# Attention in a two-block transformer kernel: probabilities divided on GpSimd and turned in transpose mode, scores on 64 rows of q and k

## The reference

```python
# layer 0: latent queries over all keys and values; the context queries over the context alone
s = einsum('bqkgd,btkd->bkgqt', qblk, k) * scale
p = softmax(s, axis=-1)
o = einsum('bkgqt,btkd->bqkgd', p, v)
# layer 1: keys within 128 positions plus all context keys, and a logit per head (the sink) in the softmax
p = softmax(concatenate([where(mask, s_w, -inf), s_c, s_sink], axis=-1))
# last layer: all keys up to the query's own chunk, with a bias by relative position
p = softmax(where(valid, scores + bias, min))
```

## Time and profile before

| | us |
|---|---|
| median of 3 runs | 3030.41 (3017.93 to 3030.89) |
| the profiled execution | 3029.36 |
| its span | 3027.6 |
| TensorE busy | 2899.5 (96%) |
| VectorE busy | 1686.7 (56%) |
| GpSimd busy | 1145.4 (38%) |
| ScalarE busy | 1050.2 (35%) |
| attention of layer 0 | 191.7 to 333.7 |
| attention of layer 1 | 1136.5 to 1326.3 |
| attention of the last layer | 2227.4 to 2295.6 |

### The profile page before, as it was taken

How to read it: one execution, slowest core, us unless ns; L and a number is a source line. 1 busy time by engine, 2 the same in 40 slices (tenths; PEclk the granted TensorE clock), 3 DMA queues, 4 the chain that set the end, 5 groups by cost and what they waited for, 6 DMA issues and landing times.

```text
span 3027.6 us, 43720 instructions
## 1 busy us (share of the span) xinstructions
PE 2899.5 (96%) x15898; PEld 2441.1 (81%) x15898; DVE 1686.7 (56%) x2794; ACT 1050.2 (35%) x1926; POOL 1145.4 (38%) x782
## 2 busy tenths in 40 slices
PE   8889999999999979999999999999999979899998
PEld 6779878888888769987888878888788758688886
DVE  5577886555545667775555564444544674432223
ACT  3247332111111437753222242222354673222222
POOL 1333223333333153323554544544353324334443
PEclk8989999999999999999999999999999999999999
DMA  5100333323232020032444423443202212122221
GB/s 217 53 28 8 120 111 135 115 89 113 88 119 90 28 78 2 1 118 92 146 169 171 145 91 139 145 152 132 101 26 81 81 61 99 68 84 97 97 97 56
DMA packets 78454, 290.91 MB, mean 96 GB/s; under 512 B 8833, under 2 KB 8961, under 8 KB 76929
## 3 DMA queue, kind: packets, MB, share of 16 engines
q1 hardware_dynamic: 78338, 289.36, 26.8%
HBM read 287.23 MB, written 2.10 MB: 96 GB/s over the span
## 4 chain that ended last, share of the span: by engine, by line
PE 85%; DVE 10%; ACT 3%; issue 1%; POOL 1%; DMA 0%; ACTq 0%; DVEq 0%; SPq 0%; POOLq 0%
PE ps L294 68%; PE ps L1258 4%; PE ps L1241 4%; PE ps L1271 3%; PE ps L494 2%; PE ps L350 1%; DVE ps L601 1%; PE ps L1516 1%; PE ps L1244 1%; DVE xl L608 1%; DVE rec L1711 1%; PE ps L955 1%; DVE r_g L1703 1%; DVE qn L1084 1%; PE ps L947 1%
## 5 line engine op out<-in xcount | busy, mean ns | idle before, releaser
L271 POOL TENSOR_TENSOR w_lo<-raw,w_hi 128x1024 fp32r<-128x1024 f32 x367 | 929.2, 2540 | 1445.4 <-ACT w_hi L265 1445.4
L265 ACT ACTIVATE w_hi<-raw 128x1024 fp32r<-128x1024 f32 x367 | 384.1, 1057 | 1355.0 <-PE ps L294 1251.1
L294 PE MATMUL ps<-n_hi,w_hi 128*128 128x512 f32 x1504 | 594.5, 395 | 12.4 <-DVE n_lo L1742 4.9
L294 PE MATMUL ps<-n_hi,w_lo 128*128 128x512 f32 x1504 | 587.4, 391 | 0.0
L294 PE MATMUL ps<-n_lo,w_hi 128*128 128x512 f32 x1504 | 587.4, 391 | 0.0
L820 DVE TENSOR_TENSOR y<-y,ps 128x512 f32<-128x512 f32 (+1 forms) x440 | 270.9, 633 | 266.1 <-PE ps L294 266.0
L339 DVE CUSTOM_DVE_ANT_0 dump<-modraw 128x1024 f32<-128x1024 f32 x212 | 356.9, 1683 | 13.8 <-DMA modraw<-mod_stream 7.9
L294 PEld LDWEIGHTS ps<-n_hi,w_hi 128*128 128x128 f32 x1504 | 283.7, 189 | 81.3 <-issue 11.7
L775 DVE TENSOR_TENSOR ps<-ffn_silu,ps 128x512 f32<-128x512 f32 x110 | 68.5, 641 | 481.0 <-PE ps L294 464.8
L294 PEld LDWEIGHTS ps<-n_lo,w_hi 128*128 128x128 f32 x1504 | 283.8, 189 | 60.6 <-issue 2.9
L294 PEld LDWEIGHTS ps<-n_hi,w_lo 128*128 128x128 f32 x1504 | 283.5, 189 | 59.3
(11 more groups left out here) (292 smaller groups left out, 4287.1 us busy)
## 6 DMA issues: line engine op xcount, KB each, us to landing
raw<-w_stream SPq DMA_DIRECT2D x367, 512.0 KB, 3.4
modraw<-mod_stream SPq DMA_DIRECT2D x152, 512.0 KB, 3.2
mod_pair<-mod_first SPq DMA_DIRECT2D x7, 1024.0 KB, 12.5
xl<-x_in SPq DMA_DIRECT2D x1, 2048.0 KB, 7.6
out<-xl SPq DMA_DIRECT2D x8, 256.0 KB, 2.0
xc<-ctx_in SPq DMA_DIRECT2D x1, 1024.0 KB, 9.7
modraw<-mod_first SPq DMA_DIRECT2D x1, 1024.0 KB, 14.9
rel<-rel_in SPq DMA_DIRECT2D x1, 1024.0 KB, 4.7
```

Of the source, the lines that this page charges most:

```text
L265: nc.scalar.activation(w_hi[:, c % RING, :], raw[:, c % RING, :], ACT.Copy).then_inc(hi_ready, 1)
L271: nc.gpsimd.tensor_tensor(w_lo[:, c % RING, :], raw[:, c % RING, :], w_hi[:, c % RING, :].bitcast(F32), ALU.subtract).then_inc(lo_ready, 1)
L294: mm = nc.tensor.matmul(out, w[a], x[b][:, off:off + n], start=first and i == 0, stop=last and i == 2)
```

## The change

- `att_stage` and `att_pool_first` are gone. The score products take q directly, on the 64 partitions of the unit's head (`rows`), and k on the same 64 partitions.
- GpSimd divides the probabilities in place by the row sum (`divide`), for each unit; the diagonal is gone. TensorE turns the blocks with `nc.tensor.transpose` against the identity.
- The sink is no exponential of its own: one more product of a 128x128 matrix of ones with a column that has the sink in its first row writes it as a last column of the scores. Row maximum, exponential and row sum take it along.
- The loops are written out; units are counted through (`i`). GpSimd makes the output's remainder two pairs behind, where it was three.
- Layer 0's twelve modulation sums stand one by one, in every fourth step.
- `ready` makes TensorE wait in layer 1 for the q chunk that a unit reads. The values are as before.

```diff
     def att_pe(pe, a, free):
...
+            rows = slice(half * HD, (half + 1) * HD)
...
-                    mm = nc.tensor.matmul(score(u, col, w), (qs_hi, qs_lo)[x][:, qt % 2, half, :],
-                                          a["k"][z][:, kc, kcol:kcol + w], start=i == 0, stop=i == 2 and not added)
+                    mm = nc.tensor.matmul(score(i, col, w), a["q"][y][rows, qc, q0:q0 + P], a["k"][z][rows, kc, kcol:kcol + w],
+                                          start=j == 0, stop=j == 2 and not added)
...
+            if a["sink"]:
+                n = a["sink"](c, x)
+                mm = nc.tensor.matmul(score(i, score_width(a, i) - 1, 1), ones[:, :], sinks[:, n:n + 1], start=True, stop=True)
...
-                    mm = nc.tensor.matmul(ps[:, 4 + g, (b - b0) * P:(b - b0 + 1) * P], prob[:, u % 2, b * P:(b + 1) * P],
-                                          dg[:, u % 2, :], start=True, stop=True)
+                    mm = nc.tensor.transpose(ps[:, 4 + g, (b - b0) * P:(b - b0 + 1) * P], prob[:, i % 2, b * P:(b + 1) * P], ident)
...
-            nc.vector.reciprocal(rinv[:, e:e + 1], rsum[:, e:e + 1]).then_inc(a["s_diag"], 1)
-            dve.wait_ge(a["s_diag"], done + a["d_steps"] - 1)
-            nc.vector.tensor_scalar(dg[:, u % 2, :], ident, rinv[:, e:e + 1], None, ALU.mult).then_inc(a["s_diag"], 1)
+        def inverse(i):
+            dve.wait_ge(a["s_p"], i + 1)
+            nc.vector.reciprocal(rinv[:, i % 4:i % 4 + 1], rsum[:, i % 4:i % 4 + 1]).then_inc(a["s_rinv"], 1)
...
+        def divide(i):
+            pool.wait_ge(a["s_rinv"], i + 1)
+            w = P * len(a["units"][i][1][4])
+            nc.gpsimd.tensor_scalar(prob[:, i % 2, 0:w], prob[:, i % 2, 0:w], rinv[:, i % 4:i % 4 + 1], 0.0, ALU.mult,
+                                    ALU.add).then_inc(a["s_norm"], 1)
...
+        for i in range(a["n"]):
+            divide(i)
+            if i % 2 and i // 2 >= M_BEHIND:
+                mixed_lo(i // 2 - M_BEHIND)
...
-        def att_mods(c, u):
-
-            if u in ATT_MODS:
-                c = MOD_FIRST + (0 if c == 0 else len(ATT_MODS)) + ATT_MODS.index(u)
-                mod_block(dve, c, [modv_a[m][:, c:c + 1] for m in range(2)], dump_att[:])
+        def att_mods(i):
+
+            if i % ATT_MOD_EVERY == 1:
+                c, m = MOD_FIRST + i // ATT_MOD_EVERY // 2, i // ATT_MOD_EVERY % 2
+                mod_block(dve, c, [modv_a[k][:, c:c + 1] for k in range(2)], dump_att[:], only=m)
...
-        in_pool(pool, l1_in, lambda pool: att_pool_first(pool, l1_att, lambda eng: eng.wait_ge(l1_in["lo"], 4)))
+        in_pool(pool, l1_in)
```

More of the change, by code:

```diff
@@ L336, in mod_block @@
         dve.wait_ge(mod_landed[slot], 16 * (turn + 1) + i * (n // MOD_RING * 16))
-        for m in range(each):
+        for m in range(each) if only is None else (only,):
             dve.wait_ge(mod_ops, ops + m + i * (each * n))
@@ L1176, in pool_dve, with attention @@
             ins.then_inc(st["mix_lo"], 1)
-    def attention(name, units, q, k, v, out, qchunk, kchunk, vcol, outchunk, next_block, extra=None, sink=None,
-                  unroll=False):
+    def attention(name, units, q, k, v, out, qchunk, kchunk, vcol, outchunk, next_block, ready, extra=None, sink=None):
+        whole = [(c, x) for c in range(ATT_ITERS) for x in units]
         groups = []
-        for x in units:
+        for _, x in whole:
             nb = len(x[4])
@@ L1196, in attention @@
                     **{"s_" + s: sem(f"{name}_{s}") for s in (
[L1197 removed]
+                        "qk", "negm", "p", "rinv", "norm", "t", "hi", "lo", "pv", "o", "m_hi", "m_lo")})
     ATT_ITERS = 4
[L1200 to L1227, removed]
-    def att_pe(pe, a, free):
[L1230 to L1237, removed]
+    def score(i, col, n):
+        return flat[:, (i % 2) * 1024 + col:(i % 2) * 1024 + col + n]
@@ L1251, in turn @@
[L1251 to L1256, removed]
+        def turn(i):
+            pe.wait_ge(a["s_norm"], i + 1)
+            for g, (b0, b1) in enumerate(a["groups"][i]):
+                if i > 0:
+                    pe.wait_ge(a["s_lo"], a["cum"][i - 1] + min(g + 1, len(a["groups"][i - 1])))
@@ L1274, in values @@
             mm.then_inc(a["s_pv"], 1)
-        def body(c, first, last):
-            for u in range(nu):
-                n = ahead(a, c, u, last)
-                if n:
-                    qk_next(c, u, n)
-                turn(c, u, first)
-                n = behind(a, c, u, first, 1, nu)
-                if n:
-                    values(*n, first)
-            if last:
-                values(c, nu - 1, False)
-        free(pe)
-        qk(0, 0)
-        qk(0, 1)
-        att_loop(pe, a, body)
@@ new lines, in att_pe, with exps, out @@
+        qk(0)
+        qk(1)
+        for i in range(a["n"]):
+            if i + 2 < a["n"]:
+                pe.wait_ge(a["s_p"], i + 1)
+                qk(i + 2)
+            turn(i)
+            if i >= 1:
+                values(i - 1)
+        values(a["n"] - 1)
+    def att_act(act, a):
+        def exps(i):
+            act.wait_ge(a["s_negm"], i + 1)
+            w, e = score_width(a, i), i % 4
+            nc.scalar.activation(prob[:, i % 2, 0:w], score(i, 0, w), ACT.Exp, bias=negm[:, e:e + 1],
+                                 accum_out=rsum[:, e:e + 1]).then_inc(a["s_p"], 1)
+        def out(i):
+            p, half = i // 2, i % 2
+            act.wait_ge(a["s_pv"], i + 1)
+            if half == 0 and p >= 2:
+                act.wait_ge(a["s_m_lo"], p - 1)
+            nc.scalar.activation(opair[half * HD:(half + 1) * HD, p % 2, :], head_out(i), ACT.Copy).then_inc(a["s_o"], 1)
```

244 lines of the change are left out of this document (89 added, 155 removed).

## The result

The changed kernel takes 3061.64 us, the median of 13 runs (3026.91 to 3075.56), against 3020.76 (3016.03 to 3030.98, 13 runs) for the kernel before: a ratio of 1.0108, 95% interval 1.0080 to 1.0135. The ratio compares means and leaves out two runs of the changed kernel that lie over 1.5% above its fastest; the two medians stand at 1.0135. It is slower, where 2989 was forecast and 3052 was the end of the range. Its profiled execution took 3061.64 us, 32.3 more than that of before.

The account below looks back on a forecast made before the run. TensorE was taken to bound all three attention stages, narrowly still after the change. Stage terms of -21, -13.7 and -6.3 us gave -41 on 3029.4: 2988, or 2989 as a median, range 2962 to 3052.

Parts of the forecast that it names:

- Scores on 64 rows: Attention score products: halving their rows was taken to cost 0, with 352 row changes bounded between 0 and 0.36 us each.
- rival 1: Attention stages: row changes drain TensorE, 352 at 0.26 us, +92 us, 3081 us; decides from 0.12 each; 12%.
- The clock: Start of layer 1's attention: 3.4 us at the low clock level after TensorE idles, costing 1.7 us.
- Rival 2: Attention: 64-row scores and transposes stream too little to hold the clock; +170 us in layer 1 alone, 3160 us; 8%.
- Transposes: Turning 592 probability blocks: one 0.111 us transpose replaces two half products each, saving 65.7 us (24.9, 32.0 and 8.9 by stage).
- The sink: Layer 1: one extra product per unit, 64 x 2 halves at 0.121 us, adds 15.4 us on TensorE.
- The division: GpSimd: 1.4 us for 768 columns, hidden in full steps; exposed at stage starts and, for 1.8 us, mid layer 0.
- Rival 3: GpSimd paces the attention: its division takes 2.7 us and holds up steps, 3004 us; 15%.
- rivals 4 and 5: Turning blocks: transposes cost as much as the products replaced, 3050 us, 5%; or run at value products' pace, 2973 us, 10%.
- Entry to layer 1: Layer 1's first scores start earlier, but q's last-chunk sum slows: +2.0 against some 1.8 us, net +0.2.

Follow-up runs that it names:

- e5: Changed kernel with unused products of ones at the stage entries and layer 1's mask products behind all score products of a unit; 3008.20 us.
- e6: Changed kernel with masked q copies back on GpSimd and score products on 128 rows; transposes, division and sink product stay; 2968.76 us.
- e2: Changed kernel with score products on all 128 rows of unmasked q and k, so not the reference's attention; 2970.67 us.
- e1: Changed kernel with unused products of ones where TensorE idles at the entries of the attention stages; 3025.32 us.
- e15: Changed kernel plus, ahead of layer 1's attention, 60 products of ones, then 40 cycles of six 64-row score products and a 128-row mask product; 1.16 us a cycle.
- e16: Like e15, but added score products also on all 128 rows, so no rows change among the added products; 0.82 us a cycle.
- e9: Changed kernel plus 300 unused transposes ahead of layer 1's attention, before the wait for q and masks, clock at 1.00; they took 32.9 us.
- e10: Changed kernel plus 150 unused 32-bit products on 64 rows ahead of layer 1's attention, begun at clock 1.00; 0.22 us each.
- e14: Changed kernel plus, ahead of layer 1's attention, 60 products of ones on 128 rows, then 240 score products on 64 rows; clock 1.00 through them.
- e11: Changed kernel plus 300 unused transposes ahead of layer 1's attention, after 12.2 us of idle time; clock back after 4.5 us.
- e13: Changed kernel plus 150 unused 32-bit products on 128 rows ahead of layer 1's attention, after idle time; clock back in 5.1 us.
- e12: Changed kernel plus 150 unused 32-bit products on 64 rows ahead of layer 1's attention, after idle time; clock not back in 64 us.

## Why the prediction was wrong

**Scores on 64 rows: "so I take 0".** This is the step that failed. A change of rows was bounded between 0 and 0.36 us, and the lower end was taken because a change of columns is free in the earlier trace rows. It measured 0.08 to 0.15 us, by stage: 8.1 us in layer 0, 7.2 in the last, and in layer 1 some 28 (e5's 191.0, plus the 9 of its saved changes, less e6's 168.2, and less the 4.2 us by which e6 waits longer ahead of the stage and not inside it), 43 us for 352 changes, 0.12 each. The steps of layer 1 at the full clock show the bare price: 2.51 us in e2 and 2.83 in after with two changes, 2.65 and 3.28 with four, 0.16 each. Layer 0 loses 0.28 in a full step, but less over the stage: beside the context units the turns of e2 start some 0.3 us after the last score product and not 0.12, behind VectorE's remainder or GpSimd's division, and its steps are up to 2.08 us long where after has 1.97. The 43 us are just the point from which rival 1 said it decides (41): without the clock the change would have been worth nothing, as e1 shows (1.0002). The rival was right that changes of rows cost time, its price (0.26) was about twice too high, and its 12% far too low for something of which no row spoke. The rule that I weighed there (the Trainium skill, "TensorEngine Tiling (Array Packing)", Tiling Modes, Key Properties: changing the tiling mode drains the engine) fits e15 against e16 with 0.34 us for a pair of changes of rows; that TensorE drains, and does not lose the time otherwise, no trace shows.

**The clock.** I let 3.4 us at the start of layer 1 run at the low level, for 1.7 us, and nothing elsewhere. Measured: 16, 25 and 85 us, worth 36 us in the medians (after less e1), and some 8 more for the 17 us that e1 kept. Not all of it comes with the changes: e2, without any, has 15 us in layer 1, where e6, which masks q and starts its scores 4.2 us later, has 4. By the traces that belongs to the idle time after the early scores, which the prediction saw, but for which it took 3.4 us of low clock. In after:

```profile
1121.11 0.58 PE L1221 MATMUL ps<-l_k_hi,l_q_hi 64*128 64x256 f32 x1 [3.42 <-ACT prob L1271]
```

Rival 2 had the place right and the cause wrong: it blamed little streaming in transposes and 64-row products as such, while e9, e10 and e14 hold 1.00 and e15 falls. Its size was wrong too, 170 us in layer 1: in the middle of layers 0 and 1, where value products and transposes stand between the changes, the clock did not fall in any trace. Why it falls in e15 and not there wasn't tested. The Trainium skill, "TensorE: Matmul & The Clock Gate", Part 4, says that transposes do not count as busy in the same way; the traces of e9 and e11, with 300 of them at 1.00 and a return after 4.5 us, do not agree.

**The two together.** After's profiled execution, stage by stage against e2's, lost 13.7, 33.5 and 44.6 us to the rows and the clock; the other parts had gained 26.7, 18.4 and 8.0 (e2 against before, with the waits ahead of layer 1).

**Transposes.** Right: 592 records, 0.109 us apart (e9: 300 in 32.9 us, the last one's own length included; 0.111 taken), full steps of 2.84 us in e2 (2.85 forecast).

**The sink.** 10.3 us instead of 15.4. The term was mis-sized: the 1.93 us of the earlier trace rows hold the last product's own length (the next group starts 1.78 us after the first, 0.111 a half), and in e6 the two halves of a sink product take TensorE 0.19 us and not 0.24, start to start:

```profile
1191.46 0.33 PE L1230 MATMUL ps<-loaded,ones 128*128 128x1 f32 x2
1191.65 0.52 PE L1240 MATMUL ps<-loaded,prob 128*128 128x128 f32 x3
```

That makes 12 us of the 64 products. For the other 2 us, that what left VectorE and ScalarE in exchange was not free in every step would explain it, and wasn't shown.

**The division.** 0.91 us for 768 columns instead of 1.4. In after there are no waits in the middle of layer 0, for which I had put 1.8 us, and none to speak of in the last stage (2); TensorE waited for it once, at the end of layer 0:

```profile
322.34 0.65 PE L1237 MATMUL ps<-loaded,prob 128*128 128x128 f32 x2 [1.10 <-POOL prob L1339]
```

That the stalls did not come and the sink product was cheaper is why e2 gained 53 us in its stages, where I had 41: 5.7 more in layer 0, 4.7 in layer 1, 1.7 in the last. Rival 3 is ruled out by the 0.91 us, and rivals 4 and 5 by the 0.109.

**Entry to layer 1.** Right but for its clock. What the scores no longer waited for came back behind them, in the pause of 3.42 us shown above, which e6 does not have. The weight split moved beside the sum of q's last chunk, which took 2.76 us (2.74 in the earlier trace rows):

```profile
1115.23 2.35 POOL L269 TENSOR_TENSOR w_lo<-raw,w_hi 128x1024 fp32r<-128x1024 f32 x1
1115.37 2.76 DVE L1082 TENSOR_TENSOR qraw<-qraw,tsh 128x512 f32<-128x512 f32 x1 [1.23 <-POOL tsh L1124]
```

## What to carry to other kernels

Before products are put on fewer rows, count how often TensorE changes between row ranges (0.17 to 0.34 us a pair here, where GpSimd had done the masking for nothing), and let the mask and bias products stand together. An operation of which the trace has no row deserves the middle of its bounds and not the end that a similar row suggests, above all when the break-even lies inside. Where a stage starts after idle time, look in several executions at how long the granted clock takes to come back; a few microseconds of unused products on all rows are a cheap cure.

## What the runs showed of the hardware

- A change of rows costs TensorE 0.16 us in the steps of layer 1 and 0.17 in e15 against e16, at the full clock.
- Changes of rows can make the granted clock fall from 1.00 to 0.50 although TensorE has work throughout (e15: within 6 us, still low 95 us later), while neither 64 rows (e14) nor transposes (e9) did; in the middle of the stages of layers 0 and 1 it did not fall in spite of the changes.
- After idle time, 32-bit products on 128 rows brought the clock back in 5.1 us (e13; 4.5 and 5.0 in e14 and e16) and transposes in 4.5 (e11), the same products on 64 rows not in 64 (e12, one execution). Why they hold it (e10) and did not raise it stays open; score products (fp32r) on 64 rows after idle time weren't tried.
- A transpose of a 32-bit block needs one load and one stream, 0.109 us (e9), where a product of 32-bit values needs two of each, 0.22 us (e10, e13).
- GpSimd multiplies with one input and a scalar column at 1.2 to 1.35 ns a column (768 in 0.91 us, 512 in 0.69), below the 2.5 to 3.5 ns of its rows with a second tile as input.
